# Two transformer blocks on one core: attention tiles from activations that are not normed yet, and a compression dealt out among projection tiles

## The reference, cut to what matters

```python
h = rms_norm(x, norm1_w[l])                 # block 1
cols = split_cols(h @ w_in[l], IN_SIZES)    # convolution, sparse, latent and stick-breaking attention
...
kc = rms_norm(compress_tokens(kc_raw, ...), kn[0])   # 31 blocks of 32 tokens, flattened, @ w1, silu, @ w2
vc = compress_tokens(vc_raw, ...)
...
n = rms_norm_2(h, norm_mix)                 # block 2
proj = n @ w_in_2                           # q_r, forget gates, values, q_a, k_a, v_a, gates
```

## Time and profile before

| | |
|---|---|
| median of 3 runs | 1916.95 us (1916.5 to 1921.07) |
| the profiled execution's own time | 1922.77 us |
| its span in the profile | 1920.9 us |
| TensorE busy | 1822.8 us (95%) |
| VectorE, ScalarE, GpSimd busy | 938.4, 698.9, 209.9 us |
| mean granted TensorE clock | 0.962 |

### The profile page before, as it was taken

How to read it: one execution, slowest core, us unless ns; L and a number is a source line. 1 busy time by engine, 2 the same in 40 slices (tenths; PEclk the granted TensorE clock), 3 DMA queues, 4 the chain that set the end, 5 groups by cost and what they waited for, 6 DMA issues and landing times.

```text
span 1920.9 us, 21029 instructions
## 1 busy us (share of the span) xinstructions
PE 1822.8 (95%) x8142; PEld 1387.9 (72%) x8142; DVE 938.4 (49%) x1682; ACT 698.9 (36%) x1264; POOL 209.9 (11%) x171
## 2 busy tenths in 40 slices
PE   4989999998999999998899989998999999999997
PEld 3657756655788888886666668885687888888885
DVE  3343245533545333334444478884445466556333
ACT  4343223454433232233344445553234332223222
POOL 3342100000200000002000033330110200000001
PEclk7998879989999999999999999999999999999998
DMA  6242201013233232232211101111421223232221
GB/s 165 84 125 88 88 1 45 23 66 110 66 120 108 88 101 97 88 109 77 88 45 45 55 23 55 55 56 45 153 88 45 66 95 103 88 103 94 90 86 44
DMA packets 122196, 152.24 MB, mean 79 GB/s; under 512 B 8779, under 2 KB 110561, under 8 KB 121458
## 3 DMA queue, kind: packets, MB, share of 16 engines
q1 hardware_dynamic: 118288, 137.85, 22.6%
q0 software_dynamic: 2112, 10.71, 1.6%
q10 hardware_dynamic: 1698, 2.35, 0.4%
HBM read 144.90 MB, written 6.00 MB: 79 GB/s over the span
## 4 chain that ended last, share of the span: by engine, by line
PE 89%; DVE 3%; ACT 2%; issue 2%; POOL 2%; ACTq 1%; POOLq 0%; DVEq 0%
PE bank L1804 47%; PE bank L1856 14%; PE bank L1182 3%; PE bank L1570 3%; PE bank L1133 2%; PE bank L2057 2%; PE bank L2060 2%; PE bank L1044 2%; PE bank L2162 2%; PE bank L2133 1%; POOL acc L826 1%; PE bank L750 1%; PE bank L1052 1%; PE bank L1946 1%; PE bank L1831 1%
## 5 line engine op out<-in xcount | busy, mean ns | idle before, releaser
L1804 PE MATMUL bank<-act_high,w_high 128*128 128x512 f32 x1344 | 548.9, 408 | 14.2 <-DVE act_low L861 9.4
L1804 PE MATMUL bank<-act_high,w_low 128*128 128x512 f32 x1344 | 528.2, 393 | 0.0
L1804 PE MATMUL bank<-act_low,w_high 128*128 128x512 f32 x1344 | 528.0, 393 | 0.0
L633 ACT ACTIVATE w_high<-ring 128x1024 fp32r<-128x1024 f32 x222 | 234.1, 1056 | 603.6 <-PE bank L1804 407.0
L657 DVE TENSOR_TENSOR w_low<-ring,w_high 128x1024 fp32r<-128x1024 f32 x202 | 254.0, 1259 | 238.5 <-ACT w_high L633 238.5
L1804 PEld LDWEIGHTS bank<-act_high,w_high 128*128 128x128 f32 x1344 | 255.5, 190 | 86.4 <-issue 26.6
L1804 PEld LDWEIGHTS bank<-act_low,w_high 128*128 128x128 f32 x1344 | 256.1, 191 | 53.6 <-issue 5.0
L1804 PEld LDWEIGHTS bank<-act_high,w_low 128*128 128x128 f32 x1344 | 254.9, 190 | 55.1
L1856 PE MATMUL bank<-act_high,w_high 128*128 128x512 f32 x416 | 162.0, 389 | 2.3 <-DVE arena L2924 1.2
L1856 PE MATMUL bank<-act_high,w_low 128*128 128x512 f32 x416 | 161.9, 389 | 0.0
L1856 PE MATMUL bank<-act_low,w_high 128*128 128x512 f32 x416 | 161.8, 389 | 0.0
(11 more groups left out here) (326 smaller groups left out, 2283.4 us busy)
## 6 DMA issues: line engine op xcount, KB each, us to landing
ring<-in_ffn_w SPq DMA_DIRECT2D x32, 1024.0 KB, 5.4
ring<-in_w_in SPq DMA_DIRECT2D x28, 1024.0 KB, 5.3
ring<-in_w_up SPq DMA_DIRECT2D x22, 1024.0 KB, 5.1
ring<-in_w_down SPq DMA_DIRECT2D x11, 1024.0 KB, 4.9
ring<-in_w_mem_kv SPq DMA_DIRECT2D x8, 1024.0 KB, 5.3
ring<-in_cmp_w SPq DMA_DIRECT2D x4, 1024.0 KB, 7.8
ring<-in_w_out SPq DMA_DIRECT2D x4, 1024.0 KB, 5.3
ring<-in_w_mix_out SPq DMA_DIRECT2D x4, 1024.0 KB, 5.2
```

What stands on the lines that cost most here:

```text
L633: nc.scalar.activation(part(w_high, name), raw_part(name), ACT.Copy).then_inc(w_rounded, 1)
L1804: last = nc.tensor.matmul(b[0:rows, :], w[:, k, 0:rows], a, start=k == 0 and n == 0, stop=k == KT - 1 and n == 2)
```

## The change

It has four parts.

1. **First norm late.** `nt` for block 1 is split from `x * g` without the factor (`gained_high` on ACT, `gained_low` on DVE). The squares are summed by TensorE directly, eight matmuls `square_sum` (L816 of the changed file) in place of POOL's sum and one matmul, the last two of them behind tile `cq0`. The factor goes to a buffer of its own, `in_rb`, and DVE, not ACT, evicts block 1's projection tiles and multiplies by it (`take_normed`, `take_query`, `take_raw_pairs`; two more multiplications in each gated convolution). The copies of x are DVE's too. Two constant transfers of POOL come later.
2. **Compression dealt out.** `features_and_compress` puts two compression matmuls behind each k step of a projection tile, four times (`a_b0`, `a_b1`, `s_q1`, `s_k1`). `memss` moves behind `a_u1`.
3. **Stick-breaking values.** `s_v0`, `s_v1` are made by `features` like the rest, and transposed by TensorE within the attention, at its units 2 and 4 (`svt0`, `svt1`).
4. **Block 2's attention tiles.** `nt` is split from `x * g` while the down projection ends; `qa0` to `va` come from it, DVE multiplies them by `rb` at eviction; while `va` runs, `nt` is renewed tile by tile with the normed activations (`mix_whole`, `mix_high_again`, `mix_low_again`), which `qr0` and all after it use. The ones-matmul of the norm stands behind `qa0`.

```diff
+        def square_sum(eng, k):
+            eng.wait_ge(big_sq, k + 1)
+            nc.tensor.matmul(bank[BIG_BANK][:, :], ones, tile(sq, k % 2), start=k == 0, stop=k == 7).then_inc(big_add, 1)
...
+            for k in range(4):
+                turn_input(k)
+            square_sum(eng, 0)
+            square_sum(eng, 1)
+            eng.wait_ge(cols_in, 16 * len(column_loads))
...
+            square_sum(eng, 2)
+            square_sum(eng, 3)
+            for k in range(4, 8):
+                turn_input(k)
+                if k > 5:
+                    square_sum(eng, k - 2)
...
             features("cq0", big="in1")
+            square_sum(eng, 6)
+            square_sum(eng, 7)
...
+            def features_and_compress(name, kv, half):
...
+                for k in range(KT):
+                    features(name, ks=(k,))
+                    if k == 0:
+                        slot_ready(eng, f"cmp{kv}{half}")
+                    m = k // 4
+                    for jw in (2 * (k % 4), 2 * (k % 4) + 1):
+                        j = 8 * half + jw
+                        last = nc.tensor.matmul(b[:, 32 * m:32 * m + N_CMP], w[:, jw * 256 + m * P:jw * 256 + (m + 1) * P],
+                                                blk[:, j, :], start=m == 0 and j == 0, stop=m == 1 and j == 15)
...
             turn_query(3)
-            compress(0, 0)
+            b = open_tile(eng, "memss")
...
             norm_sums(eng, "mk2")
-            features("a_b0")
-            compress(0, 1)
+            features_and_compress("a_b0", 0, 0)
             norm_sums(eng, "mk3")
-            features("a_b1")
+            features_and_compress("a_b1", 0, 1)
...
-            tokens_wide("s_v0", "s_v0", (0, 1))
-            tokens_wide("s_v1", "s_v0", (2, 3))
+            features("s_v1")
...
             down("dn", "h", "wd", 32)
-            big_total(eng, "mix")
             for h in range(4):
                 features(f"qa{h}", big="mix" if h == 0 else None)
+                if h == 0:
+                    big_total(eng, "mix")
...
+            def take_normed(name, dst, rows=P):
                 b = filled(eng, name)
+                nc.vector.tensor_tensor(dst, b[0:rows, :], in_rb[0:rows, :], ALU.mult).then_inc(taken_dve, 1)
...
             for k in range(KT):
                 add_to_residual(f"dn{k}", k)
+                if k == 5:
+                    split_on_dve(eng, w_part_at["qa0"])
+                if k:
+                    gained_low(eng, "mix", k - 1)
+            gained_low(eng, "mix", 7)
             split_on_dve(eng, w_part_at["qa1"])
-            big_apply(eng, "mix")
+            eng.wait_ge(big_rb, big_at["mix"] + 1)
+            for i in range(5):
+                name, dst = (f"qa{i}", ar(QA + i)) if i < 4 else ("ka", ar(K_RAW))
+                b = filled(eng, name)
+                nc.vector.tensor_tensor(dst, b[:, :], rb[:, 0:S], ALU.mult).then_inc(taken_dve, 1)
+                split_on_dve(eng, w_part_at["qa2"] + i)
+                for k in range(2 * i, min(2 * i + 2, KT)):
+                    mix_whole(eng, k)
+            for k in range(KT):
+                mix_low_again(eng, k)
```

More of the change, by code:

```diff
@@ L506, in two_blocks @@
             for i in range(2):
-                split(f"{t}{i}", t, P * i, last="s_v1" if t == "s_v" else None)
+                split(f"{t}{i}", t, P * i)
         for m in range(8):
@@ L626, in round_weights @@
                 slot_ready(eng, w_parts[i][0])
-                if i >= PAIRS and name not in LAST_PARTS:
-                    last = w_parts[i - PAIRS][3]
+                if name not in LAST_PARTS and pair_at[name] >= PAIRS:
+                    last = w_parts[w_part_at[in_pairs[pair_at[name] - PAIRS]]][3]
                     if isinstance(last, int):
@@ L891, in nt_free @@
                 eng.wait_ge(nt_read, 7 * LAST_TILES.index(name) + k + 1)
-        def big_round(eng, name):
-            for k in range(8):
-                eng.wait_ge(big_tmp, 8 * ("in1", "mix").index(name) + k + 1)
-                nc.scalar.activation(nt(k)[0], big_before(k), ACT.Copy).then_inc(big_high, 1)
         def big_ready(eng, name, k):
@@ L1800, in features @@
                         in_parts(eng, f"{parts}{k}")
+                    if name == "qr0":
+                        eng.wait_ge(mix_low, k + 1)
                     a_high, a_low = nt(k)
@@ L1817, in turn_tokens @@
                 last.then_inc(tile_filled, 1)
-            def tokens_wide(name, first, ts, halves_of=(0, 1)):
-                if 0 in halves_of:
-                    open_tile(eng, name)
-                    eng.wait_ge(w_split, w_part_at[first] + 2)
-                b = bank[bank_at[name]]
-                high, low = part_pair(w_high, first), part_pair(w_low, first)
-                for i in halves_of:
-                    t = ts[i]
-                    for k in range(KT):
-                        a_high, a_low = nt(k)
-                        for n, (w, a) in enumerate(((high, a_high), (low, a_high), (high, a_low))):
-                            last = nc.tensor.matmul(b[:, i * 256:(i + 1) * 256].rearrange("p (b c) -> p b c", c=P),
-                                                    a[:, t * P:(t + 1) * P], w[:, k], start=k == 0 and n == 0,
-                                                    stop=k == KT - 1 and n == 2)
-                if 1 in halves_of:
-                    last.then_inc(tile_filled, 1)
             def features_whole(name, load_name, c0, w=S, src=None, big=None):
@@ L1995, in _ @@
             features("a_u0")
-            b = open_tile(eng, "memss")
-            eng.wait_ge(mem_sum, 1)
-            nc.tensor.matmul(b[:, 0:256], ones, acc[:, 0:256], start=True, stop=True).then_inc(tile_filled, 1)
             turn_query(2)
@@ L2203, in take @@
                 nc.scalar.activation(dst, b[0:rows, 0:w], func, scale=scale, bias=bias).then_inc(taken_act, 1)
[L2205 to L2206 removed]
+            for k in range(4):
                 taken(eng, f"x{k}")
                 big_square(eng, "in1", k)
[L2209 to L2213 removed]
+            eng.wait_ge(cols_out, 1)
+            for k in range(4):
+                gained_high(eng, "in1", k)
+            for k in range(4, 8):
+                taken(eng, f"x{k}")
+                big_square(eng, "in1", k)
+                gained_high(eng, "in1", k)
+                if k > 5:
+                    round_weights(eng, f"cq{k - 6}")
+            in_factor(eng)
             ahead(eng, "cq0")
[L2215 removed]
             ahead(eng, "cq1")
@@ L2288, in hidden_exp @@
                                      ACT.Exp, scale=-1.0).then_inc(hid_exp, 1)
+            ahead(eng, "a_b1")
             hidden_exp(0)
-            ahead(eng, "a_b1")
             norm_squares(eng, "mq1")
             norm_factor(eng, "mq0")
-            take("s_q0", ar(SQT), scale=0.125)
             ahead(eng, "s_q0")
@@ L2397, in _ @@
             round_hidden(eng, "h", "wd", 32, 0, "up", up_sq, lambda: square_up(31))
-            big_norm("mix", "dn", then="qa1")
-            for h in range(4):
-                take(f"qa{h}", ar(QA + h))
+            eng.wait_ge(hidden_used, 30)
+            for k in range(6):
+                if k == 4:
+                    round_weights(eng, "qa0")
+                taken(eng, f"dn{k}")
+                gained_high(eng, "mix", k)
+                big_square(eng, "mix", k)
+            taken(eng, "dn6")
+            big_square(eng, "mix", 6)
+            filled(eng, "dn7")
+            gained_high(eng, "mix", 6)
+            taken(eng, "dn7")
+            gained_high(eng, "mix", 7)
+            big_square(eng, "mix", 7)
+            round_weights(eng, "qa1")
+            filled(eng, "qa0")
+            ahead(eng, "qa0")
+            big_factor(eng, "mix")
+            for h in range(1, 4):
                 ahead(eng, f"qa{h}")
-            take("ka", ar(K_RAW))
             ahead(eng, "ka")
+            for k in range(KT):
+                mix_high_again(eng, k)
             ahead(eng, "va")
@@ L2527, in _, with take @@
             nc.vector.memset(ar(24)[:, 0:2 * P], 0.0).then_inc(cols_zero, 1)
+            def take(name, dst, rows=P, w=S):
+                b = filled(eng, name)
+                nc.vector.tensor_copy(dst, b[0:rows, 0:w]).then_inc(taken_dve, 1)
+            for k in range(4):
+                take(f"x{k}", xt(k))
             eng.wait_ge(cols_turned, 1)
             nc.vector.tensor_copy(col_sb[:, :], bank[7][:, 0:ncol]).then_inc(cols_out, 1)
+            eng.wait_ge(cols_out, 1)
+            for k in range(4):
+                gained_low(eng, "in1", k)
+            for k in range(4, 8):
+                take(f"x{k}", xt(k))
+                if k > 4:
+                    gained_low(eng, "in1", k - 1)
+            gained_low(eng, "in1", 7)
             eng.wait_ge(const_in, 16)
```

245 lines of the change are left out of this document (124 added, 121 removed).

## The result

The changed kernel takes 1901.1 us at the median of 6 runs (1891.73 to 1902.0); the kernel before, 1917.42 beside it (1913.74 to 1922.65). The ratio is 0.9906, its 95% interval 0.9888 to 0.9925: 18 us faster by the ratio, 16.3 by the medians. The forecast was 1884.5 with a range of 1868 to 1898, so it had the direction and not the size, and the time lies 3 above the range.

What follows compares the result with a forecast made beforehand. TensorE, busy for 95% of the span, was taken as the bound, losing time to waits and low clock. The terms summed to -32.5: 1890.3 from the profiled 1922.8, then 1884.5 after subtracting 5.8 for the median; range 1868 to 1898.

Steps and rivals of the forecast that it cites:

- the last one: Final step: from the profiled execution's predicted 1890.3, subtract the 5.8 by which the median lay below that execution, giving 1884.5.
- So the clock costs 9.0: Compression stretch, 153.64 to 217.67: 64.03 us at mean clock 0.84 against 55.1 at full clock.
- Start: Block 1's first norm: cq0 starts 2 earlier and takes 7.9, ending at 41.6 against 43.95: -2.3, bounds 0 and -4.5.
- Evictions to DVE: Block 1: 14.5 us more work for half-idle DVE costs TensorE 0, bound +3; if DVE is late, turn_query(3) waits.
- memss and values: Block 1: memss without its wait and at full clock, -4.65; value tiles without split wait and at full clock, -6.4.
- Compression: Block 1: dealing small products into tiles keeps the clock high, less 1.0 for switches: -8.0.
- Rival 1: Dealing out the compression brings nothing, the clock falling for another cause: 1892.5; 5 in 100.
- Attention: Two transpositions enter block 1's attention where the clock is low: +1.6, bounds 1.2 and 3.
- rival 3: The attention's low-clock spell, costing 13.3, goes away: 1871; 12 in 100.
- rival 5: Slower: the attention's low-clock spell doesn't end; 120 further us of low clock would give 1943; 2 in 100.
- Block 2: Last down matmul to qr0: 33.8 in place of 46.5, -12.7; bounds +5 for the handoff, +2 for the renewal.
- Rival 4: The handoff waits: DVE or ACT late in block 2, or DVE holding block 1's banks; +5 to +7, 1890; 14 in 100.

Runs made afterwards that it cites:

- c3: The kernel before, unchanged, run again for a second profile: 1914.74 us.
- c2: The kernel before with only each compression dealt into a plain tile (a_b0, a_b1, s_q1, s_k0): 1912.74 us, ratio 0.9966.
- a3: The changed kernel with ACT's rounding of cq0's weights moved earlier, behind the first four roundings of x: 1888.87 us, ratio 0.9845.
- a4: The changed kernel with DVE's third query rotation ahead of the first gated convolution: 1897.45 us, ratio 0.9886.
- c4: The changed kernel, unchanged, run again for a second profile: 1897.95 us, ratio 0.989.
- a1: The changed kernel with the compression's 16 small products in one row behind their tile again: 1898.02 us, ratio 0.9902.
- b1: The changed kernel with s_v1's tile dealt into the attention's units 0 to 5: 1894.46 us, ratio 0.9883.
- b2: The changed kernel with six of GpSimd's eight additions for block 2's first norm cut to one column: 1894.48 us in one execution.
- d1: The same kernel as b1, run again for another profile: 1887.68 us, ratio 0.9866.
- a2: The changed kernel with block 2's part taken back (norm applied before the six tiles, ACT evicts, nothing renewed): 1911.56 us, ratio 0.9957.
- b4: b3's three reorderings plus b1's dealing of s_v1's tile into the attention: 1874.58 us, ratio 0.9782.
- b3: The changed kernel with a3's early rounding, a4's rotation order, and a_c1's eviction ahead of a norm's multiplication: 1882.9 us, ratio 0.9835.

## Why the forecast was right in direction and wrong in size

**The failed step is the last one**, "The median of the runs, 1916.95, is 5.8 below that execution; the same difference taken from it gives 1884.5", together with the term "So the clock costs 9.0". The profiled execution of before was above its median because it had low stretches behind rows that do not come every time: c3 shows the same stretch at clock 0.99 and 9.8 us shorter. The forecast took these stretches away once as the compression's gain, and once more as the distance to the median. What is removed cannot also be subtracted as noise. 4.9 of the 16.6 missed are this, the largest single part; the other 11.7 are terms of the sum, taken in order below. Seen from the median, dealing is worth 5 to 6.5 (c2) in place of 8.0.

**Start** (-2.3 forecast, -0.4). The mechanism was right, the split of `cq0`'s weights came at 33.3 for my 32.8, and the tile ran low as it did before: 8.4 for 7.9. The two sums behind it took 1.8 at the high level, so the 0.8 that was taken off was not there. a3 shows what the term left unseen: the rounding is in ACT's queue behind x6 for no reason, and moving it gives 6.0.

**Evictions to DVE** (0 forecast, bound +3; in the profiles 2.01 of waiting, and 0.8 ahead of `a_u0`). This is the second step that failed. The prediction named the place, "Where DVE is late there, `turn_query(3)` waits", and then priced VectorE's operations as if GpSimd stood still. a4 takes the 2.01 away. The 3.4 low us behind the wait cost an estimated 1.7 more in this execution (at 0.49), but they are not the wait's for certain: with waits of 1.87 to 2.01 at this place there were no low us in c4, a1, a3, b1 and b2, 3.4 in d1 and 6.8 in a2. Ahead of `a_u0` TensorE waits 2.59 for VectorE at 132.93. The Trainium skill, "SBUF — State Buffer", section "Who interferes with whom", has the rule that I did not weigh: an operation of VectorE with two inputs in SBUF and one of GpSimd that reads there contend for a port that only one of them can hold, and the order of issue decides which one stands. The row of 2.77 agrees, and so do the additions `L2738`, with one input in PSUM, which keep their 0.67 beside GpSimd. For the clock behind the wait, the Trainium skill, "TensorE: Matmul & The Clock Gate", section "HAM oscillation — how this bites in real kernels", lays a fall to pauses; a4 agrees with it, and a3, with the same pause of 2.01 and clock 1.00 behind it, does not.

**memss and values.** As forecast: `memss` no longer waits, and what its stretch misses, 1.7, is about the rotation's new wait of 2.01. **Compression** in these two profiles as forecast (-14.1 with the values for -14.4), for the reason above. **Rival 1** ("dealing brings nothing") is wrong on the mean and right in a single execution without low stretches, where dealing costs 0.4.

**Attention** (+1.6 forecast, +5.7). With the 27.3 low us of before, the changed attention would last an estimated 153.6 (between 148.99 at 17.1 and 155.17 at 30.7), 1.1 more than before, so the transpositions were priced well; the other 4.6 are a spell 10.2 us longer. That was not the change's doing: a2 has the same block 1 and 17.1, c4 is the same kernel with 30.7, and the mean over eight profiles, 28.6, is about the 27.3 of before. I gave the forecast one spell with one length; it should have been an error of plus or minus 10 low us and more, in the range. The list had only a spell that goes (rival 3) and one that doesn't end (rival 5). TensorE is busy for 17.10 of 17.10 in it, as far as rows whose ends are modelled can tell, so by the Trainium skill's rule on pauses it would not come; the trace speaks against the rule here, and b4, with wide products in the same units, has clock 0.92.

**Block 2** (-12.7 forecast, -10.9). A term mis-sized: VectorE's low part at 0.74 and weight split at 1.26 were rows without GpSimd beside them; here they took up to 1.77 and 1.73. b2 gives 2.2 back. Rival 4 named this handoff, at a higher price, and the wait for DVE that the prediction named as a sign came with 0.69.

**Behind** (+1.6, forecast 0). The changed kernel has 3.4 more low us behind 937 and 6.8 more behind 1298, in both of its profiles. At 0.49 these would be 5.0, so they are cheaper here or something else gives time back. Part 4 of the change isn't needed for it: a2, without that part, takes 993.6 from `vat` to its end, for 992.5 in the changed kernel and 990.9 before. The cause stays open, as does the place of b1's second group.

## What to carry to other kernels

Profile the same kernel twice before pricing a low clock: what differs between the two is noise of this kernel, and belongs in the range, not in the sum, and never both in the sum and in the distance to the median. Price an operation of VectorE with what GpSimd does at that moment, above all where TensorE asks for its result within a us. A thin stretch of small matmuls is worth filling with a wide tile from next to it: it bought 8.3 us at the median (b3 to b4), and runs that agree; in b1, without the other edits, it left two groups 20 apart.

## What the hardware showed

- The changed kernel's attention ran at clock 0.50 for 37.5 us in one execution and for 30.7 in another, and a kernel with the same block 1 for 17.1, TensorE busy throughout.
- A wait of TensorE of 2.01 us at one place was followed by no low us (a3, b1), by 3.4 (the changed kernel, d1) or by 6.8 (a2).
- An operation of VectorE on 128 x 510 with two inputs in SBUF (0.75 alone) took 2.77 beside GpSimd's subtraction on 128 x 1024, and one on 128 x 512 up to 1.77 beside its additions on 128 x 512; one with an input in PSUM kept its 0.67.
- Rows of 16 float32 matmuls with 31 columns left 20.4 low us behind them in one execution and none in the next.
- Two executions of the kernel before differ by 8.0 us: 9.8 less from `memss` to the value tiles, and 1.7 more ahead of it (144.25 and 145.97).
